# Two transformer blocks on one core: hand-overs between stages by halves of x

## What is computed

```python
# first block, l = 0 and 1
mix = hybrid_mixer(x, ...)
x = layer_norm(ALPHA * x + mix, ln_mix_g[l], ln_mix_b[l])
ff = swiglu(x, w1, w3, w2) if l == 0 else moe_swiglu(x, router, w1, w3, w2)
x = layer_norm(ALPHA * x + ff, ln_ffn_g[l], ln_ffn_b[l])
# second block
x = x + 0.5 * swiglu_ffn(rms_norm(x, ffn1_norm), ffn1_w_in, ffn1_w_out)
x = x + merged(rms_norm(x, mix_norm), mem) @ w_out     # attention, state space, memory branches
x = x + 0.5 * swiglu_ffn(rms_norm(x, ffn2_norm), ffn2_w_in, ffn2_w_out)
x = rms_norm(x, final_norm)

def layer_norm(x, g, b):
    return (x - mean(x)) * rsqrt(var(x) + 1e-5) * g + b
```

## Time and profile before

| | |
|---|---|
| median of three runs | 2448.49 us (2446.21 to 2452.64) |
| the profiled execution | 2449.29 us |
| its span, first to last instruction | 2447.5 us |
| PE busy | 2303.2 us, 94% of the span |
| DVE busy | 1571.6 us, 64% |
| ACT busy | 1151.3 us, 47% |
| GpSimd busy | 159.7 us, 7% |
| mean granted clock of PE | 0.95 of full |

### The profile page before, as it was taken

How to read it: one execution, slowest core, us unless ns; L and a number is a source line. 1 busy time by engine, 2 the same in 40 slices (tenths; PEclk the granted TensorE clock), 3 DMA queues, 4 the chain that set the end, 5 groups by cost and what they waited for, 6 DMA issues and landing times.

```text
span 2447.5 us, 31978 instructions
## 1 busy us (share of the span) xinstructions
PE 2303.2 (94%) x12173; PEld 1886.9 (77%) x12173; DVE 1571.6 (64%) x1684; ACT 1151.3 (47%) x1163; POOL 159.7 (7%) x224
## 2 busy tenths in 40 slices
PE   8987999898779999999999999999799999998998
PEld 7776788777667888888888888887588688757886
DVE  3555544456569898989898989887664219433443
ACT  1322433123156676767676767676545211213442
POOL 1010000101020000000000000000660001000000
PEclk9987999999889999999999999999899999788999
DMA  9302455440259999999999999999265444223552
GB/s 306 109 2 86 155 188 168 138 151 2 69 188 350 347 353 347 354 345 354 344 357 343 357 343 356 344 355 352 92 201 189 146 142 131 86 89 109 181 182 83
DMA packets 254773, 538.02 MB, mean 220 GB/s; under 512 B 17839, under 2 KB 146913, under 8 KB 254433
## 3 DMA queue, kind: packets, MB, share of 16 engines
q1 hardware_dynamic: 250960, 523.21, 61.0%
q0 software_dynamic: 3168, 9.86, 1.3%
q10 hardware_dynamic: 560, 3.79, 0.4%
HBM read 533.65 MB, written 3.15 MB: 219 GB/s over the span
## 4 chain that ended last, share of the span: by engine, by line
PE 91%; DVE 6%; ACT 2%; issue 1%; DMA 0%; DVEq 0%; POOL 0%; SPq 0%; ACTq 0%
PE bank L1209 8%; PE bank L1208 8%; PE bank L1212 8%; PE bank L1085 8%; PE bank L1086 8%; PE bank L1087 7%; PE bank L898 5%; PE bank L1343 4%; PE bank L1228 4%; PE bank L1223 4%; PE bank L1224 4%; PE bank L1062 2%; PE bank L894 2%; PE bank L1183 1%; PE bank L1491 1%
## 5 line engine op out<-in xcount | busy, mean ns | idle before, releaser
L1974 DVE TENSOR_TENSOR weights_lo<-ring_data,weights_hi 128x2048 fp32r<-128x2048 f32 x336 | 759.1, 2289 | 98.1 <-ACT weights_hi L1707 96.8
L1707 ACT ACTIVATE weights_hi<-ring_data 128x2048 fp32r<-128x2048 f32 x336 | 635.8, 1917 | 170.5 <-DMA ring_data<-in_moe_w 170.0
L1208 PE MATMUL bank<-weights_hi,xg_hi 128*128 128x512 f32 x896 | 357.0, 398 | 4.0 <-DVE arena L2339 2.6
L1209 PE MATMUL bank<-weights_hi,xg_lo 128*128 128x512 f32 x896 | 354.6, 396 | 0.0
L1969 DVE TENSOR_TENSOR weights_lo<-ring_data,weights_hi 128x2048 fp32r<-128x2048 f32 x99 | 228.5, 2338 | 52.1 <-ACT weights_hi L1544 52.1
L1519 ACT ACTIVATE arena<-bank 128x512 f32<-128x512 f32 (+4 forms) x170 | 78.8, 482 | 361.2 <-PE bank L898 111.9
L1212 PE MATMUL bank<-weights_lo,xg_hi 128*128 128x512 f32 x896 | 242.9, 393 | 0.0
L1085 PE MATMUL bank<-weights_hi,xT_hi 128*128 128x512 f32 x528 | 214.3, 406 | 22.2 <-DVE bank L2019 17.3
L1086 PE MATMUL bank<-weights_lo,xT_hi 128*128 128x512 f32 x528 | 210.6, 399 | 0.0
L1087 PE MATMUL bank<-weights_hi,xT_lo 128*128 128x512 f32 x528 | 210.5, 399 | 0.0
L1208 PEld LDWEIGHTS bank<-weights_hi,xg_hi 128*128 128x128 f32 x896 | 168.2, 188 | 43.0 <-issue 3.0
(11 more groups left out here) (436 smaller groups left out, 3287.1 us busy)
## 6 DMA issues: line engine op xcount, KB each, us to landing
ring_data<-in_moe_w SPq DMA_DIRECT2D x672, 512.0 KB, 4.2
ring_data<-in_ffn_w_in SPq DMA_DIRECT2D x88, 512.0 KB, 4.7
ring_data<-in_w_in SPq DMA_DIRECT2D x70, 512.0 KB, 4.8
ring_data<-in_ffn_w SPq DMA_DIRECT2D x66, 512.0 KB, 4.0
ring_data<-in_ffn_w_out SPq DMA_DIRECT2D x44, 512.0 KB, 3.9
ring_data<-in_w_out SPq DMA_DIRECT2D x24, 512.0 KB, 4.1
ring_data<-in_w_in SPq DMA_DIRECT2D x8, 396.0 KB, 4.3
ring_data<-in_w_in SPq DMA_DIRECT2D x8, 390.0 KB, 5.7
```

Source lines behind the costliest of these rows:

```text
L1208: mm(o, xg_hi[:, k, :], e_hi(at)[:, r], start=k == 0, stop=False)
L1209: mm(o, xg_lo[:, k, :], e_hi(at)[:, r], start=False, stop=False)
L1707: nc.scalar.activation(e_hi(at), ring_data[:, e_slot(at), :], ACT.Copy).then_inc(ring.hi_done, 1)
L1974: v.tensor_tensor(e_lo(at), ring_data[:, e_slot(at), :], e_hi(at), ALU.subtract).then_inc(ring.lo_done, 1)
```

## The change

Four edits. (1) In a dense stage PE begins `up(f, 0, 0)` when two of the four banks' low parts of x are made, and `up(f, 0, 1)` when all four are; the wait for the zeroed banks stands behind both, ahead of the loop. DVE makes the low parts of x as ACT's high parts come, without the wait for all four transposed banks, and zeroes the banks behind the three low parts of weights that open `steps`. (2) On ACT the row squares (and `unit_factors`) stand behind the three high parts that open `steps`. (3) The first two low parts of `ffn1` are made in the tail of the expert stage, around the first of its two last additions; those of `ffn2` behind the merged transpose, ahead of the additions of the output projection. (4) A layer norm is taken by halves of 512 columns, both tiles, with one signal for each half; PE transposes two banks for each.

```diff
+            def transpose_halves(src, u):
+                for q in range(2):
+                    pe.wait_ge(sem("ln_done"), 2 * u + q + 1)
+                    turn_bank(2 * q, src, 2 * q)
+                    turn_bank(2 * q + 1, src, 2 * q + 1)
@@ PE, dense
+                pe.wait_ge(sem("xT_lo"), 4 * u + 2)
+                up(f, 0, 0)
+                pe.wait_ge(sem("xT_lo"), 4 * u + 4)
+                up(f, 0, 1)
                 pe.wait_ge(sem("y_zeroed"), u + 1)
-                up(f, 0, 0)
-                up(f, 0, 1)
                 steps(f)
@@ PE, the same for every norm; waits for all of xT_lo ahead of dense are gone
-            transpose_tiles(T_FFN1, x, sem("ln_done"), 3)
-            actT_arrived(T_FFN1)
+            transpose_halves(x, 3)
             dense(ffn1, 1)
@@ ACT
             def steps(f, r=0, late=None, between=None):
                 for at in (f.up_at(1), f.up_at(1) + 1, f.down_at(0)):
                     high(f, at, r)
+                if between:
+                    between()
-            row_squares(0, ffn1, sem("ln_done"), TT * 4)
-            unit_factors()
-            dense(ffn1, memory_squares)
+            def first_row():
+                row_squares(0, ffn1, sem("ln_done"), 2 * 4)
+                unit_factors()
+            dense(ffn1, memory_squares, first_row)
-            row_squares(3, ffn2, sem("x_mixed"), 4)
-            dense(ffn2)
+            dense(ffn2, None, lambda: row_squares(3, ffn2, sem("x_mixed"), 4))
@@ DVE, split_xT
-                dve.wait_ge(sem("xT_psum"), turned_before(u) + 4)
@@ DVE, dense: what stood ahead of steps is now its "between", behind three low parts
+                def between():
+                    dve.wait_ge(sem("xT_lo"), 4 * (u + 1))
+                    for b in range(4):
+                        i = v.memset(bank[b][:, :], 0.0)
+                        if b < 3:
+                            st.do(i)
+                    i.then_inc(sem("y_zeroed"), 1)
+                    if f.row is not None:
+                        row_factor(f)
+                steps(f, 0, between, late)
@@ DVE, layer_norm
+                for q in range(2):
+                    c = slice(512 * q, 512 * q + 512)
+                    for j in range(TT):
+                        st.do(v.scalar_tensor_tensor(x[:, j, c], src[:, j, c], mv[:, j, 0:1], lnp[:, 0, c], ALU.subtract, ALU.mult))
+                    st.settle()
+                    for j in range(TT):
+                        i = v.scalar_tensor_tensor(x[:, j, c], x[:, j, c], rstd[:, j:j + 1], lnp[:, 1, c], ALU.mult, ALU.add)
+                        if j == 0:
+                            st.do(i)
+                    i.then_inc(sem("ln_done"), 1)
+                dve.wait_ge(sem("ln_done"), 2 * (u + 1))
@@ DVE, tail of the experts
                 turn(last, True)
+                low(ffn1, 0)
                 add(last + 1, 0)
+                low(ffn1, 1)
                 add(last + 1, 1)
@@ DVE, branches
                 xT_out(T_MERGED)
+                low(ffn2, 0)
+                low(ffn2, 1)
@@ DVE, main order
-            low(ffn1, 0)
-            low(ffn1, 1)
             split_xT(T_FFN1, xT2_lo, gain(R2_FFN1))
-            low(ffn2, 0)
-            low(ffn2, 1)
             split_xT(T_FFN2, xT2_lo, gain(R2_FFN2))
```

More of the change, by code:

```diff
@@ L1080, in mixer @@
                 out((2, 3, 0, 1), last=True)
-                transpose_tiles(3 * l + 2, x, sem("ln_done"), 2 * l)
+                transpose_halves(x, 2 * l)
             def three(o, x_hi, x_lo, w_hi, w_lo, start, stop, **kw):
@@ L1494, in _ @@
             mixer(0)
-            actT_arrived(T_FFN)
             dense(ffn, 0)
-            transpose_tiles(3, x, sem("ln_done"), 1)
+            transpose_halves(x, 1)
             mixer(1)
@@ L1511, in _ @@
                 turn_bank(b, x, b)
-            actT_arrived(T_FFN2)
             dense(ffn2, 2)
@@ L1566, in step, with steps @@
                 high(f, f.down_at(c), r)
-            def steps(f, r=0, late=None):
+            def steps(f, r=0, late=None, between=None):
                 for at in (f.up_at(1), f.up_at(1) + 1, f.down_at(0)):
                     high(f, at, r)
+                if between:
+                    between()
                 if f.row is not None:
@@ L1579, in steps, with dense @@
                     step(f, c, r, c + 1 < f.chunks)
-            def dense(f, late=None):
-                steps(f, 0, late)
+            def dense(f, late=None, between=None):
+                steps(f, 0, late, between)
                 silu(f, f.chunks - 1)
```

## The result

| | before | changed |
|---|---|---|
| median | 2447.01 us (five runs) | 2426.63 us (five runs) |
| profiled execution | 2449.29 us | 2426.25 us |
| its span | 2447.5 us | 2424.5 us |
| mean granted clock | 0.950 | 0.956 |

The ratio of the two is 0.9927, with a 95% interval of 0.9908 to 0.9946. Predicted were 2428.1 us. In a later comparison the changed kernel had a median of 2431.51 us against 2450.2, ratio 0.9917 (0.9896 to 0.9937). The slower ones are those with the lower mean granted clock: 0.957 at 2423.0 us, 0.952 at 2435.1 and 2435.3.

A forecast was written before the change was run, and what follows sets the result against it. TensorE was taken as the bound (91% of the span), with its idle time at five hand-overs to be won. A 5.2, B 0.35, C 0.3, D 5.1 and E 9.5 sum to 20.4 us, giving a median of 2428.1; range 2421 to 2436.

The forecast's parts named there:

- A: Hand-over into the first dense stage: first product at 240.45 against 245.63, 5.2 us gained.
- D: Hand-over into the second dense stage: first product at 1730.15 against 1735.26, 5.1 us gained.
- E: Hand-over into the third dense stage: first product 7.65 us sooner, 9.5 in all with the clock staying at 2.4 GHz.
- B: Hand-over into the second mixer: eight transposes run under the norm's second half, 0.35 us gained.
- C: Hand-over into the router, same form as B: 0.3 us gained.
- rival 2: Clock up sooner in A and D, zeroed banks then ending last: 24.5 us in all, 2424.0 us; 20%.
- the norm by halves: Layer norms: a pair of 512-column steps takes 1.30 us, the whole norm 0.28 more; bounds 0.0 and 0.6 more.
- The term of 2.5 lost at the additions: In D, low parts of weights among the last additions make the norm's statistics begin 2.5 us later.
- the banks would be level with the end of chunk 0: In E, banks zeroed at 2248.7, chunk 0 ending at 2248.65.
- 4 (lead given back): Something late for the second chunk by 5 or more in D and E: 10 us left, 2438 us; 6%.
- 5 (banks late): Slower: the wait for zeroed banks becomes the bound in three dense stages, 2464 us at three times the low parts; 2%.
- 3: Less of each: clock in E falls (1.85 less), halved norms cost 0.6 more; 17.4 us gained, 2431 us; 15%.

The follow-up runs named there:

- second profile of before: The kernel before, run once more without any edit to get another profile; 2451.29 us.
- the run with the banks ahead: Changed kernel with the four memsets and PE's wait for them ahead of the first product again, so no half start; 2441.72 us, ratio 0.9982.
- changed, second: The changed kernel, run once more without any edit to get another profile; 2432.65 us.

## Why the prediction was right, point by point

*The sum.* Predicted 20.4 us. The medians differ by 20.4 (18.7 in the later comparison), the first two spans by 23.0, and the stages that the change touches give, over all profiles, A 6.1, D 5.3, E 9.3 and B and C together -0.3, which is 20.4 too. The first two spans' 23.0 has 4.8 in the branches, 1.2 in mixer 1 and -2.8 in C that no step of mine had; but for 0.14 in C they are the clock's, of either sign. That the medians hit the sum to the tenth is luck: over its twelve times the changed kernel's median is 4.9 higher.

*A, 5.2.* The first product came 5.20 sooner after the norm's start. Two errors cancelled: the norm took 5.63 us and not 5.28, so that the second group of transposes began 5.69 behind the norm's start and not 5.30, but the first product followed 1.62 after that and not 2.03. The remaining 0.8 to 0.9 us up to the turn is rival 2, in part: the clock rose with some four products made in two of three profiles, with nine or ten in the third, and before with eight or more. The argument against rival 2, that in B transposes had not raised the level, was drawn from one profile. In the second profile of before they did, alone:

```profile
439.22:446.05 6.83, 3.33 (x16) 3.27 (x16) 5.01 (x5) 0.65 (x2) 1.05 (x2) 0.50 0.35 125
446.05:449.00 2.95, 2.12 (x13) 1.91 (x12) 1.28 (x5) 0.55 (x1) 0.00 (x0) 1.00 0.87 281
```

The 16 matmuls of the first window are the transposes, which began at 442.71; the projection began at 447.12, at the upper level. In the first profile they ran from 445.03 to 448.71 and the level stayed at 0.50 from 443.63 to 453.87. The banks of A were zeroed 0.5 us ahead of the silu, no wait; the forecast had 1.6.

*B, 0.35, and C, 0.3.* Wrong in sign, -0.14 each. The failed term is the norm by halves, at its upper bound and a little over: four pairs of 1.41 where the sum had 1.30. The overlap that I had let a pair have is there; what was too small is the price of a short step, which I had taken from an addition (0.69). The first step of each kernel, changed and before:

```profile
233.64 0.75 DVE L2070 SCALAR_TENSOR_TENSOR x<-x,small,lnp 128x512 f32<-128x512 f32 x1
```
```profile
233.12 1.28 DVE L2052 SCALAR_TENSOR_TENSOR x<-x,small,lnp 128x1024 f32<-128x1024 f32 x1
```

Two steps of 0.75 take 1.41, two of 1.28 take 2.48: about 0.08 of overlap in both. The Trainium skill, VectorE: DVE Perf Modes, on the trn2 erratum, has a fixed time for each instruction; the rows agree, with 0.75 for a step of 512 columns and 1.28, not 1.50, for one of 1024.

*D, 5.1.* 4.9 at the first product in the first profiles, 3.7 against the second of before. The term of 2.5 lost at the additions measured 2.1 against the first profile of before and 3.4 against the second, in which the scatter's matmuls ran at the upper level; undone by itself it gave 3.3. From the first product to the turn the clock gave 0.5 to 1.5 more (19.2 and 19.6 before, 18.2 to 18.75 changed). I weighed the low parts only against their old place; the timeline had 6.7 us of idle ACT and DVE ahead of Y_hi.

*E, 9.5.* 7.60 at the first product (7.65), 1.6 to 1.8 from the clock (1.85). The low parts were hidden, wholly: alone on the kernel before they gave 3.3. Of the other 4.3, 3.9 are the memsets and half of the split (the run with the banks ahead), and the rest is DVE splitting x as ACT's pieces come (its first piece 0.62 us behind the last addition instead of 1.06). That the banks would be level with the end of chunk 0 was right as well: they cost 0.25 us. The row squares' new place behind three high parts was never undone by itself; at the old place they would stand ahead of the high parts that the banks wait for.

*Rivals.* 4 (lead given back) did not happen, and 5 (banks late) only in E, by the 0.25 us above: leads at the turns were carried to the last addition of each dense stage within 0.1 us. 3 was right on the norm and wrong on the clock in E.

*What was not in the range of my reasoning* is that the other 95% of the kernel do not stand still: stretches with the same instructions move by 3 to 7 us. The range of 2421 to 2436 holds all twelve times, but mostly through the 2 to 3 us that the spread of the runs of before had added to it.

## What to carry to other kernels

Take a hand-over apart by what the next engine really needs first, and move all else behind it: here zeroing banks and half of a split cost 11.8 us in three places ahead of a product, and behind it 0.25 in one of them. Look for the idle stretch of an engine that ends before the path reaches it, rather than one beside the path, when work is to be moved: both low parts fitted where DVE was idle for 6.7 us, and cost 3.3 one wait later. Splitting a step to start its reader sooner pays only if the reader isn't kept by the rest of the split anyway; for layer norms in halves it came out even. And compare stages, not only totals, when a difference is below the spread of one kernel's times.

## What the runs showed of the hardware

Idle time of PE at a hand-over costs more than the hand-over: 99 matmuls with unused results, in time that PE had spent idle in A to D, made the kernel 13 us faster, with the stages behind them at 2.4 GHz for longer. Idleness of 1.31 us left the level up in E; after 2.88 us it fell, when PE was already at work again; seven matmuls inside 8 us of idleness put the fall off in A and left every length as it was; in A it fell with gaps of 0.76 and 1.68 us among work too, and with gaps of 0.31, 0.53 and 0.23 it did not, while in B it stayed up with gaps of 1.27 and 1.06. No length of a gap alone sorts these cases. Transposes on PE can raise the level by themselves (B, second profile of before), and the same transposes in another execution didn't. And one program, profiled three times, spent 228.8, 231.8 and 235.6 us in mixer 1 with equal instructions. That busy PE shortens exactly mixer 1 is shown; at which of its several drops in the clock the time is saved was not traced one by one. In mixer 0, ahead of every edit, the length differs by 7 us with the granted clock too: 228.90 us at a mean of 0.93 (low parts of ffn1 sooner) and 236.05 at 0.89 (changed, second), over the same 1840 matmuls. Why the level falls more often in one execution than in the next stays open.
